# Experts of 64 rows and of 128 rows visited in turn, each kind with a ring of three weight matrices

## The reference, cut to what matters

```
for e in range(N_EXPERTS):
    act = jax.nn.silu(hf @ w_gate[e]) * (hf @ w_up[e])
    out = out + combine[:, e:e + 1] * (act @ w_down[e])
```

## Time and profile before

| | |
|---|---|
| median of 3 runs | 3375.06 us (3374.67 to 3376.09) |
| the profiled execution, its own time | 3381.49 us |
| its span, first to last instruction | 3379.8 us |
| mean granted TensorE clock, share of full | 0.897 |
| TensorE busy (matmul) | 2632.9 us, 78% |
| VectorE / ScalarE / GpSimd busy | 26% / 12% / 8% |
| moved by DMA | 744.57 MB, mean 220 GB/s |

### The profile page before, as it was taken

The page is one execution under the profiler, slowest core; times in us unless marked ns, Lnnn a source line. Parts: engine busy times, 40 slices in busy tenths (PEclk is TensorE's granted clock), DMA queues, the critical chain, the costliest instruction groups (busy, mean ns, idle before and its releaser), DMA issues. The chain is left out here.

```text
span 3379.8 us, 34102 instructions
## 1 busy us (share of the span) xinstructions
PE 2632.9 (78%) x11124; PEld 1356.0 (40%) x11124; DVE 871.4 (26%) x1534; ACT 415.0 (12%) x779; POOL 279.9 (8%) x415
## 2 busy tenths in 40 slices
PE   6996779768985998867775999649699837777692
PEld 4431144234433553524432444225376424433240
DVE  1221253000004795410000000160357520000004
ACT  1011140000001001000000000010055100000000
POOL 3001140200001000020000000000000010000001
PEclk8998878898997998879997999869899959999796
DMA  9426611779954112279997899442001149999783
GB/s 345 135 78 222 210 13 57 292 315 343 335 218 142 50 50 77 75 279 421 423 423 305 323 333 338 166 137 75 0 13 36 33 177 418 423 423 422 273 296 118
DMA packets 150429, 744.57 MB, mean 220 GB/s; under 512 B 13552, under 2 KB 15264, under 8 KB 101168
## 3 DMA queue, kind: packets, MB, share of 16 engines
q1 hardware_dynamic: 100784, 592.46, 45.3%
q0 software_dynamic: 35568, 115.04, 9.9%
q10 hardware_dynamic: 13968, 35.66, 2.8%
HBM read 664.24 MB, written 79.46 MB: 220 GB/s over the span
## 5 line engine op out<-in xcount | busy, mean ns | idle before, releaser
L681 PE MATMUL ps<-w_ring,arena 128*64 128x256 f32 x3136 | 369.1, 390 | 133.3 <-DMA w_ring<-in_e_up 59.7
L604 PE MATMUL ps<-w_ring,arena 128*128 128x512 f32 x960 | 429.4, 602 | 7.2 <-ACT arena L600 7.2
L232 PE MATMUL ps<-x_feat,w_ring 128*128 128x512 f32 (+1 forms) x1152 | 421.5, 528 | 7.9 <-ACTq L145 3.7
L681 PEld LDWEIGHTS ps<-w_ring,arena 128*64 128x64 f32 x3136 | 221.5, 140 | 285.2 <-DMA w_ring<-in_e_gate 91.8
L232 PEld LDWEIGHTS ps<-x_feat,w_ring 128*128 128x128 f32 x1152 | 220.6, 192 | 208.0 <-issue 192.9
L604 PEld LDWEIGHTS ps<-w_ring,arena 128*128 128x128 f32 x960 | 183.3, 194 | 227.0 <-issue 222.5
L706 PE MATMUL ps<-w_ring,arena 128*64 128x512 f32 x784 | 182.3, 607 | 41.0 <-DMA w_ring<-in_e_down 35.4
L626 PE MATMUL ps<-w_ring,arena 128*128 128x512 f32 x480 | 211.3, 593 | 2.3 <-ACT arena L621 2.3
L324 PE MATMUL ps<-w_ring,x_feat 128*128 128x512 f32 x448 | 198.4, 606 | 13.7 <-ACTq L145 12.1
L955 PE MATMUL ps<-w_ring,fcol 128*2 128x512 f32 x384 | 182.0, 630 | 3.2 <-issue 2.3
L690 DVE TENSOR_TENSOR arena<-arena,ps 128x256 f32<-128x256 f32 x49 | 20.7, 421 | 629.9 <-PE ps L681 629.9
(11 more groups left out here) (272 smaller groups left out, 2326.9 us busy)
## 6 DMA issues: line engine op xcount, KB each, us to landing
w_ring<-in_e_gate SPq DMA_DIRECT2D x63, 2048.0 KB, 17.5
w_ring<-in_e_up SPq DMA_DIRECT2D x63, 2048.0 KB, 17.9
w_ring<-in_e_down SPq DMA_DIRECT2D x63, 2048.0 KB, 17.2
w_ring<-in_ada_w SPq DMA_DIRECT2D x24, 2048.0 KB, 10.2
w_ring<-in_w_gate SPq DMA_DIRECT2D x16, 2048.0 KB, 10.7
w_ring<-in_w_up SPq DMA_DIRECT2D x16, 2048.0 KB, 10.4
w_ring<-in_w_down SPq DMA_DIRECT2D x16, 2048.0 KB, 8.6
arena<-expert_rows ACTq DMA_DIRECT2D x39, 512.0 KB, 8.6
```

Of the source, the lines that this page charges most:

```text
L232: mm = nc.tensor.matmul(pair(j)[:, t0:t1], w[:, k, c0:c0 + P], x_feat[:, k, t0:t1], start=k == 0, stop=k == KT - 1)
L604: mm = nc.tensor.matmul(bank(2 + part), blk_feat[:, s, k, :], chunk_view(slot, FF)[:, k, :], start=k == 0, stop=k == KT - 1)
L681: mm = nc.tensor.matmul(bank(2 + part)[self.H * c:self.H * (c + 1), 0:256], blk_feat[:, s, i, self.H * h:self.H * (h + 1)], w[:, h, i, 256 ...
```

## The change

One loop takes the place of the two. Each turn does one single and then one double, on every engine, with two turns in the loop body (four visits, as before). The barrier between singles and doubles is gone. The loop runs as many turns as the larger of the two fixed counts: 16 turns of a single and a double in moe1, 32 in moe2, 32 in moe3. A kind whose visits are used up goes through its `Else` branch in every further turn.

Each kind has three slots of its own. Doubles use `w_ring` slots 0 to 2. Singles use `w_ring` slot 3, the first 4096 columns of `x_feat` and the first 4096 columns of the region `rows`. Gate and down matrices no longer rotate through all slots: visit 0 puts gate in slot 0 and up in slot 1, every later gate goes to slot 2, every later up to slot 0, every down to slot 1. Each kind counts its used matrices by its own semaphore `free`, and each slot has a `landed` semaphore. A matrix may be issued when the matrix three before it of the same kind has been used. Four matrices, not two, are issued before the scatter is complete. Rows, features and hidden values of singles have small buffers of their own (`half_rows`, `half_feat` and so on), and their outputs use bank 7. Banks 0 to 4 are shared, so TensorE waits for the other kind's `silu`, `hid` and `feat` counts. The last scale rows move to `last_rows`.

```diff
-        self.chunks = 3 * (self.doubles + self.singles) + 4
+        self.turns = max(self.doubles, self.singles) // 2
...
         class Singles:
-            def slot(self, slot, part):
-                return w_ring[:, slot, :].rearrange("p (h n) -> p h n", h=2)
+            def slot(self, slot):
+                return (w_ring[:, RING - 1, :], feat_slot, rows_slot)[slot]
...
+        def moe_sp(sp, name, m, w, chunks):
+            gate, up, down = w
+            sp.wait_ge(*count(f"{name}.table", 1))
+            kinds = (Singles(m), Doubles(m))
...
+            for kind in kinds:
+                for slot, (part, w) in enumerate((("gate", gate), ("up", up))):
+                    matrix = source(kind, w, 0, part)
+                    if kind.follows(slot, chunks.n) >= 0:
+                        sp.wait_ge(w_free, kind.follows(slot, chunks.n) + 1)
+                    load(kind, slot, matrix)
...
+            sp.wait_ge(*count(f"{name}.scattered", 32 * m.T))
+            with sp.Fori(0, m.turns) as turn:
+                for b in range(2):
+                    i = turn * 2 + (b + 1)
+                    for n, kind in enumerate(kinds):
...
+                        with sp.If(i < n_used[n]):
+                            matrix = source(kind, gate, i, "gate")
+                            freed(1)
+                            load(kind, 2, matrix)
+                            matrix = source(kind, up, i, "up")
+                            freed(2)
+                            load(kind, 0, matrix)
...
+                        with sp.If(i < n_used[n] + 1):
+                            matrix = source(kind, down, i - 1, "down")
+                            freed(3)
+                            load(kind, 1, matrix)
...
+        def moe_blocks_pe(pe, name, m):
+            kinds = (Singles(m), Doubles(m))
...
+            turn_rows(0, 0, 16)
+            pe.wait_ge(*count(at(0, "feat"), 1))
+            turn_rows(1, 0, 16)
+            for part in range(2):
+                gate_or_up(0, 0, part, part, 1)
+            pe.wait_ge(*count(at(1, "feat"), 1))
+            turn_rows(0, 1, 16)
+            pe.wait_ge(*count(at(0, "silu"), 1))
+            gate_or_up(1, 0, 0, 0, 1)
+            pe.wait_ge(*count(at(0, "hid"), 1))
+            gate_or_up(1, 0, 1, 1, 1)
+            pe.wait_ge(*count(at(0, "feat"), 2))
+            turn_rows(1, 1, 16)
+            with pe.Fori(0, m.turns) as turn:
+                for b in range(2):
+                    s = (b + 1) % 2
+                    i = turn * 2 + (b + 1)
+                    for n in range(2):
+                        other = 1 - n
+                        with pe.If(i < n_used[n]):
+                            pe.wait_ge(*count(at(n, "feat"), i + 1))
+                            pe.wait_ge(*count(at(other, "silu"), i + n))
+                            gate_or_up(n, s, 0, 2, i)
+                            turn_hidden(n, 1 - s, i)
+                            pe.wait_ge(*count(at(other, "hid"), i + n))
+                            gate_or_up(n, s, 1, 0, i + 1)
+                            pe.wait_ge(*count(at(other, "feat"), i + 1 + n))
+                            turn_rows(n, 1 - s, turn * 16 + 16 * ((b + 2) // 2 + 1))
+                            down(n, 1 - s, i)
+                        with pe.Else():
+                            pe.drain().then_inc(summed[at(n, "free")], 2)
+                            pe.sem_inc(summed[at(n, "turned")], 1)
...
-            stage(pe, "pe", "singles1")
-            moe_blocks_pe(pe, "moe1", Doubles(MOE1), chunks)
```

More of the change, by code:

```diff
@@ L398, in moe_sems @@
                 shared(name, route_counts(m))
-                for kind, n in (("single", m.singles), ("double", m.doubles)):
-                    shared(f"{name}.{kind}", visit_counts(n))
+                for kind in ("double", "single"):
+                    for part, total in visit_counts(2 * m.turns).items():
+                        shared(name, {f"{kind}.{part}": total})
                     new_sems(f"{name}.{kind}", "stored")
@@ new lines, in moe_sp, with source, load @@
+            kinds = (Singles(m), Doubles(m))
+            n_used = [kind.used(sp) for kind in kinds]
+            def source(kind, w, visit, part):
+                e = sp.value_load(expert_of[0:1, bass.ds(visit + kind.table_at, 1)], min_val=0, max_val=m.E - 1)
+                return kind.weights(w, e, part)
+            def load(kind, slot, source):
+                dest = kind.slot(slot)
+                if len(source.shape) == 3:
+                    dest = dest.rearrange("p (h n) -> p h n", h=2)
+                sp.dma_start(dest, source).then_inc(summed[f"{name}.{kind.kind}.landed{slot}"], 16)
@@ new lines, in moe_sp @@
+            for kind in kinds:
[4 more added lines that the diff above has]
+                    load(kind, slot, matrix)
+            for kind in kinds:
+                if kind.follows(2, chunks.n) >= 0:
+                    sp.wait_ge(w_free, kind.follows(2, chunks.n) + 1)
@@ new lines, in moe_blocks_pool, with at @@
+        def moe_blocks_pool(pool, name, m):
+            kinds = (Singles(m), Doubles(m))
+            def at(n, part):
+                return f"{name}.{kinds[n].kind}.{part}"
+            n_used = [kind.used(pool) for kind in kinds]
+            first = [kind.first_row(pool) for kind in kinds]
+            for n in range(2):
+                pool.sem_inc(summed[at(n, "out_free")], 2)
+            with pool.Fori(0, m.turns) as turn:
+                for b in range(2):
+                    i = turn * 2 + b
+                    for n in range(2):
+                        with pool.If(i < n_used[n]):
+                            pool.wait_ge(*count(at(n, "y_copied"), i + 2))
+                            kinds[n].store(pool, b % 2, i, first[n], summed[at(n, "stored")])
+                            pool.wait_ge(*count(at(n, "stored"), (i + 1) * kinds[n].stored))
+                            pool.sem_inc(summed[at(n, "out_free")], 1)
+                        with pool.Else():
+                            pool.sem_inc(summed[at(n, "out_free")], 1)
@@ L1376, in _ @@
                 load_columns(sp, chunks, d["ada_w"][1], 512 * (n - 12), 512)
-            sp.wait_ge(*count("moe1.table", 1))
-            for kind in (Singles(MOE1), Doubles(MOE1)):
-                moe_sp(sp, "moe1", kind, (d["w_gate"], d["w_up"], d["w_down"]), chunks)
+            moe_sp(sp, "moe1", MOE1, (d["w_gate"], d["w_up"], d["w_down"]), chunks)
             sp.wait_ge(*count("moe1.gathered", 32 * TL))
@@ L1386, in _ @@
                 load_columns(sp, chunks, d["ada_w"][1], 512 * (n - 12), 512)
-            sp.wait_ge(*count("moe2.table", 1))
-            for kind in (Singles(MOE2), Doubles(MOE2)):
-                moe_sp(sp, "moe2", kind, tuple(d[k][0] for k in ("e_gate", "e_up", "e_down")), chunks)
+            moe_sp(sp, "moe2", MOE2, tuple(d[k][0] for k in ("e_gate", "e_up", "e_down")), chunks)
             sp.wait_ge(*count("moe2.gathered", 32 * TA))
@@ L1394, in _ @@
                 load_columns(sp, chunks, d["attn_w_out"], c0, 512)
-            sp.wait_ge(*count("moe3.table", 1))
-            for kind in (Singles(MOE3), Doubles(MOE3)):
-                moe_sp(sp, "moe3", kind, tuple(d[k][1] for k in ("e_gate", "e_up", "e_down")), chunks)
+            moe_sp(sp, "moe3", MOE3, tuple(d[k][1] for k in ("e_gate", "e_up", "e_down")), chunks)
         @block.tensor
@@ L1480, in _ @@
             stage(pe, "pe", "route1")
[L1481 to L1483 removed]
+            moe_blocks_pe(pe, "moe1", MOE1)
             stage(pe, "pe", "experts1")
@@ L1590, in _ @@
             stage(act, "act", "route1")
[L1591 to L1593 removed]
+            moe_blocks_act(act, "moe1", MOE1)
             stage(act, "act", "experts1")
```

396 lines of the change are left out of this document (171 added, 225 removed).

## The result

The changed kernel takes 3272.7 us (median of 4 runs, 3270.4 to 3275.14), the kernel before 3374.86 us beside it (median of 4, 3368.75 to 3376.09). The ratio is 0.9701, 95% interval 0.9684 to 0.9718: faster by 3.0%. The forecast was 3254 us, 19 us lower, with a range of 3222 to 3305.

What follows compares the result with a forecast made beforehand. TensorE was taken to bound each pair, DMA almost equal; before, weights bound singles and TensorE doubles. -171 + 34.5 + 15 = -121 us from the profiled 3381.5 gives 3260, median 6.4 lower: 3254 us, range 3222 to 3305.

Steps and rivals of the forecast that it cites:

- the front: Before the first visit of each mixture: later scatter and double's first rows, +15 us together, bounds 0 and 33.
- the empty visits: From last down product to gather: 30 more visits of used-up kinds at 1.15 us each, +34.5 us.
- the mixtures: First gate to end of last down product: 311, 578 and 484 us in moe1 to moe3, 171 us less together.
- The pair: A single and a double side by side: 33.9 us, bound by TensorE, instead of 38.09 us.
- The rival of DMA engines that bind at 35.9 us: In pairs, DMA engines bind at 35.9 us, 2.0 us more on 26 pairs, giving 3294 us; chance 0.17.
- Left-over singles: Singles after the pairs in moe2 and moe3: three slots suffice, so each keeps 16.14 us.
- The rival of starved slots: Left-over singles take 22.8 us each with three slots, giving 3386 us; chance 0.08 partly starved, 0.04 wholly or new wait.
- The last down product: End of each mixture: its matrix is issued only after the down product before it, costing 9 us each.
- The sign named beforehand: In the profile after, 17 to 31 us from the last down product to the gather.
- a later scatter: Two more matrices ahead, 9.9 us at 422 GB/s, delay the scatter by 1, 5 and 6 us in moe1 to moe3.
- the double's first rows: TensorE transposes them in front of the single's first gate, 1 us in each mixture.

Runs made afterwards that it cites:

- run 5: Changed kernel with the second 512 columns of a double's down product left out, all transfers kept; 3168.9 us, ratio 0.9389.
- run 4: Changed kernel with the last down matrix of a kind loaded into the free slot 2; 3241.2 us, ratio 0.9607.
- run 2: Changed kernel with loops cut to the 5, 10 and 12 turns this input needs; 3227.3 us, ratio 0.9566.
- run 7: Changed kernel with turns in which both kinds are used up passed in one branch; 3235.3 us, ratio 0.9592.
- run 1: Changed kernel with the doubles' first gate and up weights waiting for the scatter; 3263.5 us, ratio 0.9672.
- run 9: Changed kernel with no weights of either kind issued before the scatter's end; 3250.4 us, ratio 0.963.
- run 6: Kernel of run 1 with the double's first rows transposed after the single's gate and up; 3266.0 us, ratio 0.968.
- run 10: Changed kernel with the last down matrix in the free slot and used-up turns passed in one branch; 3211.1 us, ratio 0.9512.

## Why the prediction was right, and where a term was off

**The total.** The forecast of 3254 is 19 us under the measured 3272.7. Between the two profiled executions the forecast had -121.5 and measured was -111.1, 10.4 us apart: the front 15.4 too little, the empty visits 3.6 too little, the mixtures 1.5 and the other stages 7.1 the other way. The remaining 8.7 us are no part of the mechanism: the forecast took its median to lie 6.4 us under its profiled execution, as before, and it lay 2.3 us above.

**The mixtures: right, in sum and by part.** -172.5 us against -171. By the same count as in the prediction the mixtures take 310.7, 578.6 and 481.4 us, where 311, 578 and 484 stood. The pair came at 34.08 for 33.9, bound by TensorE as argued; run 5 shows the DMA floor 1 us below. The rival of DMA engines that bind at 35.9 us is refuted by the same run. Its base, 370 GB/s for a full share within doubles, took the share of a stretch that isn't full for a rate: the pairs run at 408 GB/s.

**Left-over singles: right.** 16.1 us each with three slots, at a share of 1.01. The rival of starved slots would have shown a longer period.

**The last down product: the mechanism right, the sum in part by luck.** 9 us each was forecast as a wait; measured were waits of 7.60, 6.49 and 5.83 us, and 6.5 us of products lengthened by the lower clock, which the prediction didn't have. Together 26.5 against 27, so one omission covers the other. The stretch that the prediction reasoned from, the end of one down product to the start of the last, is 10.1, 9.0 and 8.9 us, as forecast; but some of it is transposes and other idle time, and 2.2 to 2.6 us of it remain in run 4. Run 4 shows the cause of the waits by taking them away.

**Empty visits: the size holds, the model doesn't.** Forecast +34.5, measured +38.1. Runs 2 and 7 show two things that lie side by side: a floor of some 9 to 12 us, in which the last output is copied and stored and the engines meet, and TensorE's string of empty visits at 1.36 us each (12, 25 and 19 of them give 16.3, 34.0 and 25.8 us; measured 16.0, 34.0 and 25.8). The sign named beforehand, 17 to 31 us, was missed at both ends. The 1.1 was the slope from 9.6 us after 6 visits to 14.05 after 10, and the first of these lies at the floor. For 30 more visits the difference is small, since 10 visits stood just above the floor already; for fewer visits it isn't: 52 taken away in run 2 gave 44.1 us and not 71.

**The front: the term that was mis-sized.** Forecast +15, of which 12 for a later scatter and 3 for the double's first rows; measured +30.4, near the upper bound of 33. The timelines split it at the issue of the first rows:

| us | before | after | run 1 | run 9 |
|---|---|---|---|---|
| scatter begins to rows' issue, moe1 | 37.5 | 37.1 | 37.1 | 37.4 |
| moe2 | 42.0 | 47.0 | 43.2 | 34.1 |
| moe3 | 25.3 | 35.6 | 26.0 | 15.8 |
| rows' issue to first gate, moe1 | 10.9 | 15.8 | 15.7 | 16.7 |
| moe2 | 9.0 | 16.3 | 16.6 | 18.8 |
| moe3 | 11.7 | 15.1 | 19.9 | 17.3 |

The scatter's part is 14.9 us against 12. In moe3 it is 10.3, so the estimate of 9.9 us for two more matrices ahead was the value to take, and 6 was a discount that nothing bore out. The second part is 15.6 us where 3 stood, and is the step that failed. Some 10.5 us of it lie between the first transposes and the first gate, which were 1.82 us apart and are 4.71, 6.13 and 5.14 now: TensorE waits for the double's rows (1.71, 3.13, 2.14 us) and turns them (1.94 us). The other 5 are first rows that land later, in moe1 and moe2; that they wait behind matrices asked for just before is likely but not shown. Summed over the mixtures, the first part is 104.8 us before and 119.7 after, 106.3 in run 1 and 87.3 in run 9; the second part is 31.6 before and 47.2 after, 52.2 and 52.8 in runs 1 and 9. So holding weights back shortens the first part by 13 and 32 us and lengthens the second by 5 in both.

**What the prediction left out.** The stages outside the mixtures were 7.1 us shorter in the profiled execution, about 2.5 us ahead of each scatter. No edit touches them. The same stretches differ as much among the profiled executions of the other kernels: the first scatter begins between 601.6 and 607.4 us, and from the gather of moe1 to the next scatter it takes 438.1 to 442.7. So the spread of single executions is enough for the 7.1 us, and they shouldn't be counted as a gain of the change.

## What to carry to other kernels

When one kind of work is bound by transfers and the other by TensorE, alternate them, each with a small ring of its own. One after the other they cost the time of the transfers plus that of TensorE; in turns they cost the larger of all the transfers and all the products. Then look at the two ends of the loop, where most of what remained lay: transfers that are sent early to be ready can delay the one transfer that everything waits for, and the last turns need a way out that doesn't pass through every empty branch. A cost per visit that is read off two totals may hide a floor: ask what else runs beside it.

## What the hardware showed beyond that

Where large packets and small ones competed for the DMA engines here, the small ones got the smaller share of the bytes. The DMA queues in the first 12 us of moe3's scatter (packets, MB, share), in the changed kernel and then in run 9:

```profile
q1 hardware_dynamic: 343, 2.68, 55.2%
q0 software_dynamic: 340, 1.26, 32.4%
```

```profile
q0 software_dynamic: 1082, 3.97, 81.2%
```

Both queues got nearly the same number of packets, 343 and 340, but a packet of weights carries 7.8 KB on average and one of the scatter 3.7 KB. Alone the scatter moves three times as much in the same time. Over its whole length moe3's scatter of 4.19 MB took 34.3 us beside 8.39 MB of weights, 24.7 beside 4.19 MB (run 1) and 14.5 alone (run 9), so each two matrices sent ahead cost it 10 us. The Trainium skill's page "DMA: Bandwidth & Descriptors", section Queues, rings and completion order, says that each DMA engine goes round its queues packet by packet. The counts of 343 and 340 agree with taking turns; in the earlier trace rows they were 387 and 277, so less even, and equal counts are no rule shown here.

TensorE's idle time can cost more than itself: behind a wait of 6.49 us the last down product of moe2 took 6.60 us at a granted clock of 0.55, and 3.65 at 1.00 where the wait was gone (run 4). The first gate behind each front took 4.2 to 4.6 us in the changed kernel, at clocks of 0.80 to 0.87, and 5.9 us at 0.61 in run 6's moe2, instead of 3.67. A short wait is no safeguard, though: in run 10 the last down product of moe1 ran at 0.81 behind 0.77 us.
